# The first attention of a two-block transformer kernel written as one run of 64 blocks, on one core

## The reference

```python
def mla_queries(cq, q_norm_g, w_uq):
    q = (rms_norm(cq, q_norm_g) @ w_uq).reshape(b, n, N_HEADS, NOPE_DIM + ROPE_DIM)
    return q[..., :NOPE_DIM], q[..., NOPE_DIM:]          # 64 and 32 of each head

def mla_keys(kvr, kv_norm_g, w_ukv):
    c_kv = rms_norm(kvr[..., :KV_RANK], kv_norm_g)
    kv = (c_kv @ w_ukv).reshape(b, n, N_HEADS, NOPE_DIM + V_DIM)
    return kv[..., :NOPE_DIM], kvr[..., KV_RANK:], kv[..., NOPE_DIM:]

def attend(qn, qr, kn, kr, v):
    s = jnp.einsum('bqhd,bkhd->bhqk', qn, kn) + jnp.einsum('bqhd,bkd->bhqk', qr, kr)
    p = jax.nn.softmax(s.astype(jnp.float32) * ATTN_SCALE, axis=-1).astype(v.dtype)
    return jnp.einsum('bhqk,bkhd->bqhd', p, v)
```

## Time and profile before

| | us |
|---|---|
| median of 3 runs | 4174.67 (4169.2 to 4182.7) |
| the profiled execution | 4172.43 |
| its span, first to last instruction | 4170.4 |
| PE busy in it | 3762.7 (90%) |
| DVE busy | 2719.6 (65%) |
| ACT busy | 1415.5 (34%) |
| first attention, from its first product at 377.89 to the next stage's first matmul at 788.10 | 410.2 |

### The profile page before, as it was taken

The page is one execution under the profiler, slowest core; times in us unless marked ns, Lnnn a source line. Parts: engine busy times, 40 slices in busy tenths (PEclk is TensorE's granted clock), DMA queues, the critical chain, the costliest instruction groups (busy, mean ns, idle before and its releaser), DMA issues.

```text
span 4170.4 us, 48954 instructions
## 1 busy us (share of the span) xinstructions
PE 3762.7 (90%) x16080; PEld 2883.6 (69%) x16080; DVE 2719.6 (65%) x5007; ACT 1415.5 (34%) x2122; POOL 79.5 (2%) x114
## 2 busy tenths in 40 slices
PE   6787777899999998999999999789899988878998
PEld 5674444487888887778787877564578766556876
DVE  1596655547997884787777788688563446646343
ACT  2323333334333343222222232344342335524232
POOL 0000000000000000000000000000000000000000
PEclk7898888999999999999999999998999999989999
DMA  3222111132344555656565654260122222212222
GB/s 151 77 99 82 51 56 50 61 126 86 112 142 158 209 206 192 202 194 208 196 212 186 225 173 152 97 142 31 41 85 92 92 66 81 64 47 71 94 92 72
DMA packets 134713, 497.73 MB, mean 119 GB/s; under 512 B 14204, under 2 KB 14332, under 8 KB 129565
## 3 DMA queue, kind: packets, MB, share of 16 engines
q1 hardware_dynamic: 99600, 362.87, 25.7%
q0 software_dynamic: 16448, 96.48, 6.8%
q10 hardware_dynamic: 18508, 36.40, 3.1%
HBM read 429.62 MB, written 66.06 MB: 119 GB/s over the span
## 4 chain that ended last, share of the span: by engine, by line
PE 75%; DVE 12%; ACT 5%; issue 4%; DVEq 2%; DMA 1%; ACTq 0%; PEld 0%; PEldq 0%; SPq 0%; POOL 0%; POOLq 0%
PE ps L361 21%; PE ps L362 20%; PE ps L363 20%; PE ps L2386 3%; PE ps L2256 2%; PE ps L411 2%; PE ps L386 1%; DVE w_lo L344 1%; PE ps L2006 1%; DVE nmax L1595 1%; PE ps L480 1%; DVE rinv L426 1%; PE ps L2247 1%; PE ps L2068 1%; DVE rinv L1373 1%
## 5 line engine op out<-in xcount | busy, mean ns | idle before, releaser
L361 PE MATMUL ps<-RH,w_hi 128*128 128x512 f32 x2464 | 992.0, 403 | 92.4 <-DVE RL L440 45.7
L344 DVE TENSOR_TENSOR w_lo<-raw,w_hi 128x1024 fp32r<-128x1024 f32 x535 | 649.9, 1223 | 603.3 <-ACT w_hi L339 597.6
L362 PE MATMUL ps<-RL,w_hi 128*128 128x512 f32 x2464 | 971.7, 394 | 0.0
L363 PE MATMUL ps<-RH,w_lo 128*128 128x512 f32 x2464 | 970.8, 394 | 0.0
L339 ACT ACTIVATE w_hi<-raw 128x1024 fp32r<-128x1024 f32 x535 | 559.3, 1055 | 1049.0 <-PE ps L363 963.5
L361 PEld LDWEIGHTS ps<-RH,w_hi 128*128 128x128 f32 x2464 | 469.8, 191 | 227.6 <-issue 80.4
L363 PEld LDWEIGHTS ps<-RH,w_lo 128*128 128x128 f32 x2464 | 469.8, 191 | 100.2
L362 PEld LDWEIGHTS ps<-RL,w_hi 128*128 128x128 f32 x2464 | 470.6, 191 | 96.0 <-issue 3.1
L361 PE MATMUL ps<-WH,w_hi 128*128 128x512 f32 x1024 | 406.0, 396 | 30.8 <-DVE Y L1715 25.3
L362 PE MATMUL ps<-WL,w_hi 128*128 128x512 f32 x1024 | 400.1, 391 | 0.0
L363 PE MATMUL ps<-WH,w_lo 128*128 128x512 f32 x1024 | 399.9, 391 | 0.0
(11 more groups left out here) (309 smaller groups left out, 4516.5 us busy)
## 6 DMA issues: line engine op xcount, KB each, us to landing
raw<-w_all SPq DMA_DIRECT2D x536, 512.0 KB, 3.3
mod_in<-w_modr SPq DMA_DIRECT2D x128, 512.0 KB, 4.5
peer_gate_scratch<-Gs POOLq DMA_DIRECT2D x16, 2048.0 KB, 7.2
GL<-peer_gate_scratch POOLq DMA_DIRECT2D x32, 1024.0 KB, 9.1
act_scratch<-act_out ACTq DMA_DIRECT2D x80, 256.0 KB, 2.6
act_in<-act_scratch POOLq DMA_DIRECT2D x20, 1024.0 KB, 10.8
mod_up<-w_mods SPq DMA_DIRECT2D x4, 2048.0 KB, 22.2
Tb<-bias_row_scratch POOLq DMA_DIRECT2D x32, 256.0 KB, 3.1
```

The source lines that it names most:

```text
L344: nc.vector.tensor_tensor(w_lo[j][:], raw[j][:], w_hi[j][:].bitcast(F32), ALU.subtract).then_inc(lo_done, 1)
L361: nc.tensor.matmul(out_ap, w_hi[slot][:, k, :], rh, start=start and x == 0, stop=False)
L362: nc.tensor.matmul(out_ap, w_hi[slot][:, k, :], rl, start=False, stop=False)
L363: last = nc.tensor.matmul(out_ap, w_lo[slot][:, k, :], rh, start=False, stop=stop and x == n - 1)
```

## The change

The 16 heads become one run of 64 blocks, t = 0 to 63, t = 8p + n, written out in full with no hardware loop.

- PE: `scores(t+2)` is issued in block t, behind `turn(t)`, also across pairs.
- `turn(t)` is in two halves of three tiles, x = 0 in bank 4 and x = 1 in bank 5, each with its own copy by ACT (128x384 each) and its own `tp_evac`. `values` is also in halves of three tiles; in the blocks n = 0 and 4 they stand ahead of the two half turns: `values(.,0)`, `turn(t,0)`, `scores(t+2)`, `values(.,1)`, `turn(t,1)`.
- The products for pair p+1 are eight pieces, all in bank 7, one in each block from n = 1 (k = 0) to the next pair's n = 0 (k = 7): keys 512 and 256 columns, rotary queries of both heads, plain queries of both heads, values 512 and 256 columns, transposes of `VT` four and two. Each piece waits for the evacuation of the one before (`gen_out`). For the first pair all eight run at the start in eight banks.
- Queries are regrouped: the weight columns are put in another order on the host, so that one product has the 64 plain rows of both heads and one the 32 rotary rows of both heads with their swapped rows. ACT copies the plain ones with the scale (two copies of 64x512); DVE rotates both heads in two multiplications of 64x512 and two additions of 32x512 (before: eight instructions a pair). This takes a second table, `trig2`, one more load of 256 KB at the start of the program, for which ACT's first instruction waits.
- `KT`, `QT` and `Vk` have two buffers each. The rotary key rows are copied to the second `KT` once.
- DVE: in block t it does the scaling of t+1, some other work, the maximum of t+2, and some more other work (in n = 0 and 4 alone). The low part of a pair is in n = 1, the split to `w_lo` in n = 2, the sums for the modulation in n = 0, 3, 4, 5, the taps in n = 0, 4, 6, 7.
- ACT: in block t both half copies, the exponential of t+2, and then the piece's copy; in n = 1 the rounding to `w_hi` stands between, in n = 0 the copy to `RH`.

The core of the diff:

```diff
+            def turn(t, x):
+                pe.wait_ge(p_done, t + 1)
+                if t:
+                    pe.wait_ge(tp_evac, 2 * t - 1 + x)
+            for t in range(BLOCKS):
+                p, n = t // 8, t % 8
+                if n % 4 == 0 and t:
+                    values(t // 4 - 1, 0)
+                    turn(t, 0)
+                    scores(t + 2)
+                    values(t // 4 - 1, 1)
+                    turn(t, 1)
+                else:
+                    turn(t, 0)
+                    turn(t, 1)
+                    if t + 2 < BLOCKS:
+                        scores(t + 2)
+                if n == 0 and p:
+                    piece(p, 7, 7)
+                if n and p + 1 < PAIRS:
+                    piece(p + 1, n - 1, 7)
```

More of the change, by code:

```diff
@@ L158, in build @@
         ypad = at(S, "ypad", [P, KC, T + 2 * HALF_W])
[L159 removed]
+        KT = [[at(S + kb + 3 * m, f"KT{x}_{m}", [P, KEYS]) for m in range(2)] for x, kb in enumerate((17, 70))]
         CQH = at(S + 23, "CQH", [P, 2, T], F32R)
@@ new lines, in heads_out @@
+            def heads_out(p):
+                act.wait_ge(pv_done, 4 * p + 4)
+                sc.activation(RH[:, p, :], bank(6), ACT.Copy).then_inc(o_hi, 1)
+            for k in (0, 1, 3, 4, 5, 6, 7):
+                piece_out(0, k, k)
+            exponential(0)
+            exponential(1)
+            for t in range(BLOCKS):
+                p, n = t // 8, t % 8
+                turned(t, 0)
+                turned(t, 1)
+                if t + 2 < BLOCKS:
+                    exponential(t + 2)
+                if n == 0 and p:
+                    piece_out(p, 7, 7)
+                    heads_out(p - 1)
+                if n == 1:
+                    hi_ahead(act, R_MLA + p // RING, p % RING)
+                if n and n != 3 and p + 1 < PAIRS:
+                    piece_out(p + 1, n - 1, 7)
@@ new lines, in rotated @@
+            def rotated(p, b):
+                dve.wait_ge(gen_mm, 8 * p + 3)
+                v.scalar_tensor_tensor(t_sb[0][0:NOPE], ps[0:NOPE, b, :], SCALE1, trig2[0:NOPE], ALU.mult, ALU.mult)
+                v.scalar_tensor_tensor(t_sb[1][0:NOPE], ps[NOPE:P, b, :], SCALE1, trig2[NOPE:P], ALU.mult, ALU.mult)
+                dve.drain()
+                for m in range(2):
+                    rows = slice(ROPE * m, ROPE * m + ROPE)
+                    ins = v.tensor_tensor(QT[p % 2][m][NOPE:QK], t_sb[0][rows], t_sb[1][rows], ALU.add)
+                ins.then_inc(gen_out, 1)
@@ new lines, in _ @@
+            rotated(0, 2)
+            largest(0)
+            largest(1)
+            normalised(0)
+            for t in range(BLOCKS):
+                p, n = t // 8, t % 8
+                more = p + 1 < PAIRS
+                if t + 1 < BLOCKS:
+                    normalised(t + 1)
+                if n == 0:
+                    mod_sum(p, 0)
+                    conv_taps(p, 0, 2)
+                elif n == 1 and p:
+                    low_part(p - 1)
+                elif n == 2:
+                    lo_ahead(dve, R_MLA + p // RING, p % RING)
+                elif n == 3:
+                    mod_sum(p, 1)
+                elif n == 4:
+                    if more:
+                        rotated(p + 1, 7)
+                elif n == 5:
+                    mod_sum(p, 3)
+                elif n >= 6:
+                    conv_taps(p, n, n + 1)
+                if t + 2 < BLOCKS:
+                    largest(t + 2)
+                if n == 0:
+                    conv_taps(p, 2, 4)
+                elif n == 4:
+                    conv_taps(p, 4, 6)
+                    mod_sum(p, 2)
+                if n == 7 and p % 4 == 3:
+                    store_conv(6 + p // 4)
@@ L2266, in _, with scores @@
-                    turn(6)
-                    if pp < 3:
-                        generated(i, pp + 1)
-                    turn(7)
-                    if pp < 3:
-                        first_queries(i, pp + 1)
-                    values(1)
+                ins.then_inc(gen_mm, 1)
+            def scores(t):
+                p, m, b = t // 8, t // 4 % 2, t % 4
+                if t % 8 == 0:
+                    pe.wait_ge(gen_out, 8 * p + 4 if p else 8)
+                if t >= 2:
+                    pe.wait_ge(exp_done, t - 1)
+                q = QT[p % 2][m][0:QK, b * P:(b + 1) * P]
+                o = 2 * (t % 2)
+                mm(bank(o), q, KT[p % 2][m][0:QK, 0:T], start=True, stop=True)
+                mm(bank(o + 1, TC), q, KT[p % 2][m][0:QK, T:KEYS], start=True, stop=True).then_inc(s_done, 1)
@@ new lines, in _ @@
+            for k in range(8):
+                piece(0, k, k)
+            scores(0)
+            scores(1)
+            for t in range(BLOCKS):
+                p, n = t // 8, t % 8
+                if n % 4 == 0 and t:
[4 more added lines that the diff above has]
+                    turn(t, 1)
+                else:
+                    turn(t, 0)
+                    turn(t, 1)
+                    if t + 2 < BLOCKS:
+                        scores(t + 2)
+                if n == 0 and p:
+                    piece(p, 7, 7)
+                if n and p + 1 < PAIRS:
+                    piece(p + 1, n - 1, 7)
@@ L2273, in _ @@
+            values(HEADS - 1, 0)
+            values(HEADS - 1, 1)
             meet(pe, "pe", tl)
```

258 lines of the change are left out of this document (103 added, 155 removed).

## The result

The changed kernel takes 4074.37 us, median of 4 runs (4071.77 to 4075.89), against 4175.78 us for the kernel before on the same chip. The ratio is 0.9756, 95% interval 0.9739 to 0.9773. The forecast was 4073, in a range of 4050 to 4112. The profiled execution has a span of 4070.1 us; before it was 4170.4.

A forecast was written before the change was run, and what follows sets the result against it. It took DVE's loop as the new bound: 34.3 us a pair, 35.8 with queue orders. Stage 300.8 plus 7 for the clock, 308 against 410.2, gives -102, +0.6 for `trig2`: median 4073, range 4050 to 4112.

The forecast's parts named there:

- The two waits: PE in the kernel before: 48.0 us waiting for DVE's query evacuation, 46.4 us for ACT's copies of transpositions.
- DVE's loop as the bound: Scaling, maximum and exponential loop once a block through DVE: 34.3 us a pair, 35.8 with queue orders.
- 2.77 + E: DVE's step per block: 2.77 us of loop plus the block's other DVE work E, summing to 10.6 a pair.
- my hand layout of blocks 0 and 4: PE and ACT laid beside DVE's loop: late exponentials add 0.9 us in n = 0, 0.1 in n = 4.
- The clock: One fall of PE's clock in every other pair at 2 us each: 1 us a pair, 7 in all.
- The stall in n = 2: PE stalls 2.8 us for the first key piece's copy, queued behind an exponential and the 1.05 us rounding.
- The clock rival: PE's clock keeps falling as before: 40.1 us a pair, time 4098; chance 0.17.
- the exposed pieces: Each piece waits for ACT's copy of the one before, 1.3 us seven times a pair: 4138; chance 0.08.
- no gain at all: The gain is given back in a later stage or the order does nothing: 4174; chance 0.02.
- The slower one: Look-ahead of two blocks collapses, 5.1 us a block in sequence, 57 us a pair: 4228; chance 0.03.
- The faster one: No queue effects or clock falls, DVE's loop alone at 34.3 us a pair: 4056; chance 0.10.
- PE's floor of 31.8: PE's turns, scores, `values` and products need 31.8 us a pair at the higher clock; at it, 4036.

The follow-up runs named there:

- e6: Changed kernel with scores, maximum, exponential and scaling one block ahead instead of two; 4214.57 us, stage 456.1 us against 316.1.
- e7: Changed kernel with all eight pieces of the next pair together in block n = 5; stage 441.6 us against 316.1.
- e5: Changed kernel with whole six-tile turns and one copy, both `values` halves ahead of the turn in n = 0 and 4; stage 342.0 us against 316.1.
- e8: Changed kernel with DVE's four rotating instructions run twice, same values; stage 326.3 us against 316.1.
- e9: Changed kernel with ACT's rounding in n = 3 and DVE's maximum right behind the scaling except in n = 0 and 4; 4049.29 us against 4074.2.
- e1: Changed kernel with ACT's weight rounding moved from n = 1 to n = 3, DVE's split from n = 2 to n = 5; stage 306.35 us against 316.1.
- e10: Changed kernel, rounding in n = 3, maximum first everywhere; in n = 0 and 4 scores before `values`, exponential before both copies; stage 294.9 us against 316.1.
- e0: Changed kernel run again unchanged; stage 315.55 us, ratio 0.9773 to the kernel before.
- e2: Changed kernel with ACT's exponential ahead of the second half copy in n = 0 and 4; stage 313.2 us against 316.1.
- e3: Changed kernel with DVE's maximum directly behind the scaling in all eight blocks; stage 310.5 us against 316.1.
- e4: Changed kernel with later rounding, exponential before the second half copy in n = 0 and 4, and maximum first in all blocks; stage 299.2 us against 316.1.

## Why the prediction was right, step by step

**The two waits.** Both places that it named in the kernel before are gone from PE's waits. That the change works through these is shown from the other side too: without the second block of look-ahead (e6) or the spread pieces (e7) the stage is longer than before, without the half banks (e5) it is 25.9 us longer than now, without the regrouped queries (e8) 10.2. These four, 140.0, 125.5, 25.9 and 10.2, don't add up to the 94.1 gained, since each is measured with the other three in place: they are parts of one pipeline, and taking out either of two is enough to break it.

**DVE's loop as the bound.** The cost of 2.77 + E per block holds within 0.03 us in five blocks: 3.37 against 3.38 in n = 1, 3.92 against 3.93 in n = 3 (pair 4) and 3.95 in n = 5, 3.43 against 3.45 in n = 6 and 7. In n = 2 it gives 3.90, to which the split's wait adds 0.2 (forecast 0.3); the 0.2 for the low part's wait in n = 1 did not come. The 1.06 us of waiting for the exponential is in the row of nearly every reciprocal. The forecast said "about 1 us in six blocks of eight"; it is there in all eight where the clock falls, and shrinks to 0.34 in n = 4 where it doesn't. That the loop and not PE's work sets the changed kernel's pair is shown by e9: it changes no work on any engine, only what stands inside DVE's wait and where ACT rounds, and is 25 us shorter. The rounding alone (e1) gives 9.7 of them, and at a clock of 1.00 the maximum's place gives 1.9 us a pair (36.3 to 34.4). In n = 0 and 4 the loop is held from PE through ACT, as laid out in the forecast.

**The mis-sized terms.** The stage was forecast at 308 and took 316.1. By parts, in us:

```
                 forecast         measured
lead-in          15.9             16.0
pair 0           34.1             35.9
pairs 1 to 6     214.8 + 6 clock  225.7
pair 7 and tail  36 + 1 clock     38.5
```

Pairs 1 to 6 hold 4.9 of the 8.3 missing, pair 0 1.8, pair 7 1.5 (its last `values` took 6.90 at a fallen clock, where I had 5.3). The step that was mis-sized is my hand layout of blocks 0 and 4. In n = 0 its frame was right: PE did come in 2.5 us ahead of the scaling. What it does from there took 7.6 us and not 7.2. The chain has a half of `values` at 2.72 in every pair where I had 2.6, and the timelines of PE and DVE at the start of pair 1 are:

```profile
425.14 2.79 PE L2295 MATMUL ps<-PT,Vk 128*64 128x512 f32 x6
...
432.73 0.38 PE L2258 MATMUL ps<-ident,VT 128*128 128x128 f32 x2
```

```profile
427.64 0.16 DVE L1599 RECIPROCAL rrow<-psum_row 128x1 f32<-128x1 f32 x1 [1.06 <-ACT Pm L934]
```

The 0.4 goes through the half copy and the exponential into DVE's step: 6.7 for 6.3. In n = 4 DVE's own work is 7.2 (10.09 of e8 less the 2.91 from 447.31 to 450.22 that the second rotation takes there) and not 6.9, and it waits 0.34 for the exponential where I had 0.1: 7.5 for 7.0. Behind a fall of the clock PE begins the `values` of n = 4 only 0.74 us ahead of the scaling (445.51 against 446.25) and not 1.66 (557.47 against 559.13 in pair 4), and the step is longer by just that difference: 8.46.

The forecast's sum of PE's work was wrong too: **PE's pair is 33.8 us, not 31.8**, as e9 shows (202.69 over six). "The change leaves this work as it is" doesn't hold for the half turns. Of the 2 us, `values` is some 0.5, and the four half turns another 0.5: from start to start one is 0.47 where I had 0.35, as PE's timeline of e10 has it, at the higher clock:

```profile
431.43 0.55 PE L2281 MATMUL ps<-ident,Pm 128*128 128x128 f32 x3
431.90 2.79 PE L2294 MATMUL ps<-PT,Vk 128*64 128x512 f32 x6
```

The rest is in the pieces, some 0.8, and in the full turns, 0.2, by the chain of e9's pair 2 (455.33 to 489.89), which runs through PE but for 3.1 us. The first matmul of a piece takes longer than those behind it, 0.41 for 0.23 with 512 columns and 0.30 for 0.12 with 256:

```profile
471.46 0.41 PE ps L362
471.87 0.23 PE ps L363
...
486.68 0.30 PE ps L362
```

What I took for a floor 4 us under the loop is 2.5 us under the 36.3 of a pair without a fall.

**The clock.** Total right, parts wrong. I had one fall in every other pair at 2 us each. The fall came in five pairs of six and cost 1.3 us each (37.8 in a pair with one, 36.5 in the one without), 1.1 a pair against the 1.0 of the forecast. That the two agree is chance. The stall in n = 2 was forecast at 2.8 us (9.6 to 12.4 after the scaling) and is 1.74 (10.4 to 12.1), PE's timeline and the clock behind it being:

```profile
437.44 0.59 PE L2274 MATMUL ps<-KT,QT 96*128 96x256 f32 x2
439.77 0.39 PE L362 MATMUL ps<-CKH,w_hi 128*128 128x256 f32 x1 [1.74 <-ACT KT L912]
...
440.38 1.49 PE L2282 MATMUL ps<-ident,Pm 128*128 128x128 f32 x6
441.66 1.91 PE L2273 MATMUL ps<-KT,QT 96*128 96x512 f32 x2
```

```profile
439.80:443.00 3.20, 3.20 (x11) 2.38 (x12) 2.06 (x5) 2.98 (x8) 0.00 (x0) 0.60 0.02 5
...
553.00:556.50 3.50, 3.35 (x16) 2.21 (x17) 2.36 (x5) 3.26 (x9) 0.00 (x0) 1.00 0.00 0
```

The turn at 440.38 and the scores behind it take nearly twice their length at 2.4 GHz, at a granted 0.60, so mostly at 1.2 GHz; the like stretch of pair 4 has 1.00. The cause of the stall was as forecast: ACT's copy of the first key piece stood behind an exponential and the weight rounding. ACT's timeline:

```profile
436.70 0.90 ACT L934 ACTIVATE Pm<-ps,nmax 128x768 f32<-128x768 f32 x1 [0.87 <-DVE nmax L1593]
...
437.59 1.04 ACT L340 ACTIVATE w_hi<-raw 128x1024 fp32r<-128x1024 f32 x1
438.54 0.58 ACT L911 ACTIVATE KT<-ps 64x512 f32<-64x512 f32 x1
439.13 0.59 ACT L912 ACTIVATE KT<-ps 64x512 f32<-64x512 f32 x1
```

e1 takes away the rounding there and with it half of the stall and every fall in pairs 1 to 6, for 9.7 us: 7.5 of them in pairs 1 to 6 (225.7 to 218.2), 2.2 in the rest of the stage. Why pair 4 was spared, with the same stall, stays open; it was spared in e0 too. The same stall of 1.74 was followed by a fall in three pairs of six in e8, and one of 1.45 in four of six in e2 and in two of six in e3. In the Trainium skill, TensorE: Matmul & The Clock Gate, section "A second HAM failure mode: psum-queue depth-cycling", short idles between groups that cycle through PSUM banks make the clock swing. The changed kernel's clock falls and rises so in five pairs of six. e1 and e9 have such idles too, but shorter ones, and don't bear the rule out: they ran at 1.00 in all six pairs. That rule would have given 4098; it was worth 1.1 us a pair and not 4.3.

**Small steps.** The extra table `trig2` at the start, +0.6, did not show: its issue put that of the first weights 0.47 us later, and PE yet started no later (12.57 us against 12.84). The expected gain of nothing in later stages holds within the scatter given above.

**The rivals.** The clock rival (4098), the exposed pieces (4138) and no gain at all (4174) did not come. The slower one (4228) is real as a mechanism, at 4214.57 in e6, but needs one block less of look-ahead than the change has. The faster one had the right order but the wrong floor: "PE's floor of 31.8" for 4036 can't be reached, and what can be, 4049.29, is the kernel e9.

## What to carry to other kernels

When several engines run one pipeline from in-order queues, lay the queues side by side and find the loop that passes through them once a block; work that stands inside the loop's wait is free, work outside it adds to every block. Move the loop's instruction first only where its input is sure to be there: in the two blocks of eight where the scores were late, the same move cost what it had gained in the six others (e3 against e9). Compare pairs at the same clock before you credit a gain to an order: most of what e3 gained was falls that didn't come. An instruction moved ahead of another is given back by whatever waits for the one that was passed (e2), so before pricing such a move, write down who waits for the passed one; and add up the engine that seems to have slack by records of the same shape before calling it a floor.

## What the runs showed of the hardware

- A stall of PE of 1.74 us was followed by a granted clock at the lower level for part of the next blocks in five pairs of six in the changed kernel and in three of six in e8, one of 1.45 us in four of six (e2) and in two of six (e3); with stalls of at most 1.1 us (e1), 0.6 us (e4) or 0.5 us (e9, e10) the clock stayed at 1.00 in all six pairs. Before, a stall of 2.21 was not followed by a fall and one of 2.31 was the earlier trace rows. So the length of one stall alone doesn't decide.
- A fall costs little where PE has slack: 1.3 us in a pair of 37.6, and next to nothing in e8, where DVE is full in n = 4 (39.00 us without a fall in pair 1, 39.01 with one in pair 6). Where the pipeline is already broken the clock is low for long: in e6 and e7 the granted clock of the pairs was 0.82 and 0.81.
- The two profiled executions of the changed kernel have stages 0.55 us apart, while the first product of the stage, after the same code, lay anywhere between 373.95 and 378.93 us. Orders worth 3 to 10 us could be judged by the stage and not by the total.
